# A seven-product down projection whose weight sums are made by adding DMAs

## What is computed

```python
h = _rmsnorm(x, norm_mlp[l])
u = jax.nn.relu(jnp.einsum('bsd,df->bsf', h, w_up[l]))      # (1, 256, 8192)
x = x + jnp.einsum('bsf,fd->bsd', u * u, w_down[l])         # (1, 256, 2048)
return _rmsnorm(x, norm_final)
```

## Time and profile before

| what | us |
|---|---|
| median of 3 runs | 1001.91 (1000.73 to 1002.18) |
| the profiled execution's own time | 1000.99 |
| its span in the trace | 999.2 |
| PE busy | 986.5 |
| DVE busy | 586.4 |
| ACT busy | 419.6 |
| packets of the main DMA queue, as a share of 16 engines | 52.1% |
| data moved | 193.52 MB |

### The profile page before, as it was taken

How to read it: one execution, slowest core, us unless ns; L and a number is a source line. 1 busy time by engine, 2 the same in 40 slices (tenths; PEclk the granted TensorE clock), 3 DMA queues, 4 the chain that set the end, 5 groups by cost and what they waited for, 6 DMA issues and landing times.

```text
span 999.2 us, 12457 instructions
## 1 busy us (share of the span) xinstructions
PE 986.5 (99%) x5088; PEld 847.2 (85%) x5088; DVE 586.4 (59%) x428; ACT 419.6 (42%) x325; POOL 1.4 (0%) x9
## 2 busy tenths in 40 slices
PE   8999999999999999999999999999999999999996
PEld 7888888888888888888888888888888888888885
DVE  6597777655554766544656654556565445656453
ACT  6644435354443434333444433343433334444342
POOL 0000000000000000000000000000000000000000
PEclk9999999999999999999999999999999999999998
DMA  9956543555544655555455455545545554555512
GB/s 327 392 194 229 190 188 122 215 211 190 189 169 169 233 189 195 183 208 177 165 211 206 176 203 191 187 151 213 209 183 207 176 204 132 211 209 205 187 66 84
DMA packets 29694, 193.52 MB, mean 194 GB/s; under 512 B 3296, under 2 KB 3552, under 8 KB 7136
## 3 DMA queue, kind: packets, MB, share of 16 engines
q1 hardware_dynamic: 29232, 190.85, 52.1%
q10 hardware_dynamic: 288, 1.18, 0.3%
q0 software_dynamic: 144, 1.05, 0.3%
HBM read 190.97 MB, written 2.10 MB: 193 GB/s over the span
## 4 chain that ended last, share of the span: by engine, by line
PE 94%; DMA 3%; SPq 1%; DVE 1%; ACT 0%; issue 0%; ACTq 0%
PE ps L343 44%; PE ps L252 33%; PE ps L255 17%; DMA w_raw<-w_stream 3%; SPq L208 1%; PE ps L277 0%; PE ps L329 0%; SPq L193 0%; DVE w_lo L628 0%; ACT w_hi L449 0%; PE ps L317 0%; DVE val L635 0%; PE ps L276 0%; PE ps L279 0%; ACT cross L483 0%
## 5 line engine op out<-in xcount | busy, mean ns | idle before, releaser
L628 DVE TENSOR_TENSOR w_lo<-w_raw,w_hi 128x2048 fp32r<-128x2048 f32 x172 | 392.0, 2291 | 280.4 <-ACT w_hi L449 279.7
L449 ACT ACTIVATE w_hi<-w_raw 128x2048 fp32r<-128x2048 f32 x172 | 326.8, 1912 | 344.0 <-PE ps L343 210.8
L252 PE MATMUL ps<-act_a,w_hi 128*128 128x512 f32 x1472 | 351.1, 391 | 0.0
L343 PE MATMUL ps<-w_hi,act_b 128*128 128x512 f32 x1280 | 345.3, 390 | 0.0
L252 PEld LDWEIGHTS ps<-act_a,w_hi 128*128 128x128 f32 x1472 | 271.0, 188 | 52.5
L343 PEld LDWEIGHTS ps<-w_hi,act_b 128*128 128x128 f32 x1280 | 239.8, 188 | 49.3
L343 PE MATMUL ps<-w_lo,act_b 128*128 128x512 f32 x640 | 199.7, 389 | 0.0
L255 PEld LDWEIGHTS ps<-act_a,w_lo 128*128 128x128 f32 x1472 | 188.6, 191 | 7.0
L255 PE MATMUL ps<-act_a,w_lo 128*128 128x256 f32 x1472 | 191.1, 283 | 0.0
L343 PEld LDWEIGHTS ps<-w_lo,act_b 128*128 128x128 f32 x640 | 120.2, 188 | 25.0
L635 DVE TENSOR_TENSOR val<-ps,cross 128x1024 f32<-128x1024 f32 x26 | 31.8, 1223 | 47.2 <-ACT cross L455 47.2
(11 more groups left out here) (68 smaller groups left out, 164.3 us busy)
## 6 DMA issues: line engine op xcount, KB each, us to landing
w_raw<-w_stream SPq DMA_DIRECT2D x172, 1024.0 KB, 4.8
w_raw<-w_stream SPq DMA_DIRECT2D x16, 256.0 KB, 7.9
x<-x_rows SPq DMA_DIRECT2D x2, 1024.0 KB, 17.4
mix_mem<-x_t SPq DMA_DIRECT2D x3, 512.0 KB, 8.2
out<-x SPq DMA_DIRECT2D x6, 256.0 KB, 2.7
mix_mem<-pool_w ACTq DMA_DIRECT2D x1, 1024.0 KB, 9.1
mix_mem<-g_final POOLq DMA_DIRECT2D x1, 1024.0 KB, 5.0
out<-val SPq DMA_DIRECT2D x2, 256.0 KB, 2.1
```

The lines of the kernel that those rows point to most:

```text
L252: return pe.matmul(ps[:, bank, :], weights_hi, act, start=first, stop=False)
L343: mm = pe.matmul(ps[:, NT * parity + t, :], a[:, at:at + P], cols, start=first and i == 0, stop=last and i == 2)
L449: act.activation(w_hi[:, c, :], w_raw[:, c, :], ACT.Copy).then_inc(hi_ready, 1)
L628: dve.tensor_tensor(out=w_lo[:, c, :], in0=w_raw[:, c, :], in1=w_hi[:, c, :].bitcast(F32), op=ALU.subtract)\
```

## The change

The row blocks of w_down are replaced by a scheme in the manner of Strassen, with seven block products in place of eight. The 8192 features are cut into 8 slices of 1024, each slice into two groups of 512. For one slice and one half of the output columns (1024 of 2048), activations are a 2 x 2 arrangement of quadrants (two token halves by two feature groups, A11, A12, A21, A22), and the weights another (four quadrants of 512 x 512, each one chunk of 1 MiB). Such a pair is a **unit**, d = 0 to 13; it does seven products of 128 tokens x 512 features x 512 columns, each with 12 matmuls. Some operands are sums of quadrants:

- Sums of activation quadrants (S5, N6, N3, S7) are made by DVE, once for a slice, that is for two units, and are then split into hi and lo by ACT and DVE (`quad_hi`, `quad_lo`).
- Four weight operands are sums (T1 to T4). T1, T2 and T4 are built one upon another in a buffer `sums[d % 2]` in `mix_mem`: SP loads quadrant 1, then POOL issues a DMA that adds quadrant 0 (T1), later quadrant 3 (T2), later quadrant 2 (T4). T3 is made in `w_raw` slot 3 by an adding DMA of quadrant 1 upon quadrant 3, after DVE has split quadrant 3. Each add is issued when DVE has split the sum before it.
- The running product sums lie in PSUM banks 4, 5 and 6, and DVE adds or subtracts them into `x` seven times per unit (`fold`, 128 x 512 each).

From the third up block on (t = 2 to 15, d = t - 2) PE does one up block and one unit, interleaved in a **step** of 11 items: up 0, A11·B11, S5·T1, up 1, N3·B22, N6·T2, up 2, S7·T3, up 3, A12·B21, A22·T4. They are called items 0 to 10 below. All up blocks from t = 2 use banks 0 to 3. The last slice is done plainly, with eight products for each half of the columns' pair (`plain`, 8 chunks of 24 matmuls). w_up blocks keep two `w_raw` slots, the quadrants the two others; `w_hi` and `w_lo` are rings of four slots over all items.

The core of the diff (hunks and lines left out are marked "..."):

```diff
+LEAD = 2
...
+UP_AT = (0, 3, 6, 8)
+A11_B11, S5_T1, N3_B22, N6_T2, S7_T3, A12_B21, A22_T4 = 1, 2, 4, 5, 7, 9, 10
+STEPS = 11
...
+PLAINS = 8
...
+FOLDS = 7
...
+        sums = (mix_mem[:, 0:CHUNK_W], mix_mem[:, CHUNK_W:2 * CHUNK_W])
...
+            def load_up(t, c, before):
+                sp.wait_ge(lo_ready, before + 1)
+                sp.dma_start(w_raw[:, c % 2, :], w_stream[CHUNKS * (FIRST_UP + t) + c, :, :])\
+                  .then_inc(raw_loaded[c % 2], 16)
+            def load_quad(to, d, n, before, loaded):
+                sp.wait_ge(lo_ready, before + 1)
+                sp.dma_start(to, w_quads[4 * d + n, :, :]).then_inc(loaded, 16)
+            sp.wait_ge(value_ready, 2)
+            for t in range(LEAD, UPS):
+                d = t - LEAD
+                lead = d == 0
+                load_quad(sums[d % 2], d, 1, up_item(1, 0) if d < 2 else term_item(d - 2, A22_T4),
+                          sum_base_loaded[d % 2])
+                load_up(t, 0, up_item(1, 0) if lead else up_item(t - 1, 2))
+                load_quad(w_raw[:, 3, :], d, 3, up_item(1, 3) if lead else term_item(d - 1, S7_T3),
+                          raw_loaded[3])
+                load_up(t, 1, up_item(1, 1) if lead else up_item(t - 1, 3))
+                load_quad(w_raw[:, 2, :], d, 0, up_item(1, 2) if lead else term_item(d - 1, A12_B21),
+                          raw_loaded[2])
+                load_up(t, 2, up_item(t, 0))
+                load_quad(w_raw[:, 2, :], d, 2, term_item(d, A11_B11), raw_loaded[2])
+                load_up(t, 3, up_item(t, 1))
...
+            def add_quad(to, d, n, after, added):
+                pool.wait_ge(lo_ready, after + 1)
+                pool.dma_start(to, w_quads[4 * d + n, :, :], accum_op=ALU.add).then_inc(added, 16)
+            def add_to_base(d):
+                pool.wait_ge(sum_base_loaded[d % 2], 16 * (d // 2 + 1))
+                pool.dma_start(sums[d % 2], w_quads[4 * d, :, :], accum_op=ALU.add).then_inc(t1_added, 16)
+            add_to_base(0)
+            for d in range(SEVENS):
+                add_quad(sums[d % 2], d, 3, term_item(d, S5_T1), t2_added)
+                add_quad(w_raw[:, 3, :], d, 1, term_item(d, N3_B22), t3_added)
+                if d + 1 < SEVENS:
+                    add_to_base(d + 1)
+                add_quad(sums[d % 2], d, 2, term_item(d, N6_T2), t4_added)
...
+            def term(d, which, quad, bank, first):
+                g = term_item(d, which)
+                pe.wait_ge(quad_ready, quad_count(d // 2, quad))
+                pe.wait_ge(hi_ready, g + 1)
+                to = ps[:, bank, :]
+                for k in range(CK):
+                    pe.matmul(to, quads[:, quad, k, 0:P], weights_of(w_hi, g, k),
+                              start=first and k == 0, stop=False, skip_group_check=not first)
+                    pe.matmul(to, quads[:, quad, k, P:2 * P], weights_of(w_hi, g, k),
+                              start=False, stop=False, skip_group_check=not first)
+                pe.wait_ge(lo_ready, g + 1)
+                for k in range(CK):
+                    mm = pe.matmul(to, quads[:, quad, k, 0:P], weights_of(w_lo, g, k),
+                                   start=False, stop=k == CK - 1, skip_group_check=not first)
+                mm.then_inc(chunk_used, 1)
+            for t in range(LEAD, UPS):
+                d = t - LEAD
+                up_chunk(t, 0)
+                if d == 0:
+                    pe.wait_ge(summed, turn(FIRST_UP) + LEAD)
+                else:
+                    pe.wait_ge(folded, FOLDS * d)
+                term(d, A11_B11, A11, NT, True)
+                term(d, S5_T1, S5, NT + 1, True)
+                up_chunk(t, 1)
+                pe.wait_ge(folded, FOLDS * d + 2)
+                term(d, N3_B22, N3, NT + 1, False)
+                term(d, N6_T2, N6, NT, False)
+                up_chunk(t, 2)
+                pe.wait_ge(folded, FOLDS * d + 4)
+                term(d, S7_T3, S7, NT, False)
+                up_chunk(t, 3)
+                term(d, A12_B21, A12, NT + 2, True)
+                pe.wait_ge(folded, FOLDS * d + 5)
+                term(d, A22_T4, A22, NT, False)
...
+                up_hi(t, 0)
+                take_up(t - 1)
+                act.wait_ge(raw_loaded[2], 16 * (FIRST_UP + LEAD + 2 * d + 1))
+                hi_of(term_item(d, A11_B11), w_raw[:, 2, :])
+                square_up(t - 1)
+                act.wait_ge(t1_added, 16 * (d + 1))
+                hi_of(term_item(d, S5_T1), sums[d % 2])
+                if folding:
+                    act.wait_ge(part_ready, parts + 1)
+                    quad_hi(s, S5, part_0, S5_T1)
+                up_hi(t, 1)
+                if folding:
+                    act.wait_ge(part_ready, parts + 2)
+                    quad_hi(s, N6, part_1, N6_T2)
+                act.wait_ge(raw_loaded[3], 16 * (FIRST_UP + LEAD + d + 1))
+                hi_of(term_item(d, N3_B22), w_raw[:, 3, :])
+                if folding:
+                    act.wait_ge(part_ready, parts + 3)
+                    quad_hi(s, N3, part_0, N3_B22)
+                    parts += 3
+                act.wait_ge(t2_added, 16 * (d + 1))
+                hi_of(term_item(d, N6_T2), sums[d % 2])
+                if folding:
+                    act.wait_ge(squared, t)
+                    quad_hi(s, A12, val[:, :, 0:P], A12_B21)
+                    quad_hi(s, A22, val[:, :, P:S], A22_T4)
+                else:
+                    act.wait_ge(squared, t)
+                    quad_hi(s + 1, A11, held[:, :, 0:P], A11_B11)
+                up_hi(t, 2)
+                act.wait_ge(t3_added, 16 * (d + 1))
+                hi_of(term_item(d, S7_T3), w_raw[:, 3, :])
+                up_hi(t, 3)
+                act.wait_ge(raw_loaded[2], 16 * (FIRST_UP + LEAD + 2 * d + 2))
+                hi_of(term_item(d, A12_B21), w_raw[:, 2, :])
+                act.wait_ge(t4_added, 16 * (d + 1))
+                hi_of(term_item(d, A22_T4), sums[d % 2])
...
+                if d:
+                    fold(d - 1, 5, S7_T3, NT, 1, 1, ALU.subtract)
+                if folding:
+                    quad_lo(s, S7, part_2)
+                up_lo(t, 0)
+                add_up(t - 1)
+                lo_of(term_item(d, A11_B11), w_raw[:, 2, :])
+                dve.wait_ge(squared, t)
+                if folding:
+                    made(dve.tensor_tensor(out=part_0, in0=val[:, :, P:S], in1=held[:, :, P:S],
+                                           op=ALU.subtract))
+                if d:
+                    fold(d - 1, 6, A12_B21, NT + 2, 0, 0, ALU.add)
+                lo_of(term_item(d, S5_T1), sums[d % 2])
+                if folding:
+                    quad_lo(s, S5, part_0)
+                    made(dve.scalar_tensor_tensor(out=part_1, in0=held[:, :, 0:P], scalar=-1.0,
+                                                  in1=part_0, op0=ALU.mult, op1=ALU.subtract))
+                if d:
+                    fold(d - 1, 7, A22_T4, NT, 1, 0, ALU.add)
+                up_lo(t, 1)
+                if folding:
+                    quad_lo(s, N6, part_1)
+                    made(dve.scalar_tensor_tensor(out=part_0, in0=part_1, scalar=-1.0,
+                                                  in1=val[:, :, 0:P], op0=ALU.mult, op1=ALU.subtract))
+                elif s + 1 < SLICES - 1:
+                    make_s7()
+                lo_of(term_item(d, N3_B22), w_raw[:, 3, :])
+                if folding:
+                    quad_lo(s, N3, part_0)
+                fold(d, 1, A11_B11, NT, 0, 0, ALU.add)
+                lo_of(term_item(d, N6_T2), sums[d % 2])
+                if folding:
+                    quad_lo(s, A12, val[:, :, 0:P])
+                    quad_lo(s, A22, val[:, :, P:S])
+                else:
+                    quad_lo(s + 1, A11, held[:, :, 0:P])
+                fold(d, 2, S5_T1, NT + 1, 1, 1, ALU.subtract)
+                up_lo(t, 2)
+                lo_of(term_item(d, S7_T3), w_raw[:, 3, :])
+                fold(d, 3, N3_B22, NT + 1, 0, 1, ALU.subtract)
+                up_lo(t, 3)
+                fold(d, 4, N6_T2, NT, 0, 1, ALU.subtract)
+                lo_of(term_item(d, A12_B21), w_raw[:, 2, :])
+                lo_of(term_item(d, A22_T4), sums[d % 2])
```

More of the change, by code:

```diff
@@ new lines, in plain @@
+            def plain(f, halves, done):
+                g = FIRST_PLAIN + f
+                d, k2, n = PLAIN_OF[f]
+                bank = (6, 4, 0, 2)[2 * d + n]
+                of_half = ((A11, A21), (A12, A22))[k2]
+                pe.wait_ge(hi_ready, g + 1)
+                pe.wait_ge(lo_ready, g + 1)
+                for k in range(CK):
+                    for i, (at, of) in enumerate(((0, w_hi), (P, w_hi), (0, w_lo))):
+                        for t in halves:
+                            mm = pe.matmul(ps[:, bank + t, :], quads[:, of_half[t], k, at:at + P],
+                                           weights_of(of, g, k), start=k2 == 0 and k == 0 and i == 0,
```

(49 more changed lines are left out.)

245 lines of the change are left out of this document (173 added, 72 removed).

## The result

| | before | after |
|---|---|---|
| median | 1001.32 us (4 runs) | 1108.98 us (4 runs, 1105.71 to 1112.98) |
| profiled execution, span | 999.2 us | 1111.2 us |
| mean granted TensorE clock | 0.996 | 0.958 |

The ratio is 1.108, 95% interval 1.103 to 1.112: 10.8% slower. I forecast 1014 us, 1.3% slower, with a range of 970 to 1058. The direction was right, the size was not, and the range missed.

The account below looks back on a forecast made before the run. PE was taken as the bound. From the profiled 1001.0 us, 38.1 us of removed matmuls came off and 14 units x 3.6 us of stalls (50.4) were added: 1013.3, with 0.9 for the median 1014 us; range 970 to 1058.

Parts of the forecast that it names:

- Removed work: w_down products on PE: 168 fewer matmuls at 0.2268 us each save 38.1 us, all on the path.
- ACT, DVE: Added work in a 41.3 us step: ACT 27 us, hidden by PE; DVE 38.7 (even units) and 33.9 (odd).
- DVE's crowd: DVE's queue before item 4: fold 2 makes it 1.3 us late in even units, 9 us in all.
- The price of an add: Each adding DMA reads twice: 5.2 us of the engines, 7.4 us alone; T2 9.3 us with nearby loads.
- The queue of POOL: POOL issues T2, T3, next T1, T4; only adds queue behind its waits, and the base is asked for before T4.
- the T4 chain: T3, next T1 and T4 one behind another, sharing engines with four plain loads: item 10 late, 1.1 us a unit.
- Start and end at zero: First up blocks, first unit's lead-in, plain slice and last block add nothing; without their cover 1 to 2 us.
- Slow adding: Rival: addition holds the engines for 3 or 4 loads' time, DMA is the bound: 1114 or 1259 us; chance 0.14.
- Cheap adds: Rival: an add flows like a plain load, T2 lands in 5 us, only DVE's crowd is left: 973 us; chance 0.26.

Follow-up runs that it names:

- adds as cheap as loads: Changed kernel with the four adding DMAs of a unit made plain loads of the same bytes, so the sums are not formed: 987.4 us, ratio 0.987.
- the base early: Changed kernel with SP's load of the next sum base moved ahead of three other loads, order of adds kept: 1036.5 us, ratio 1.036.
- both queue edits: Changed kernel with the next sum base loaded earlier and T4's add issued before the next unit's T1 add: 1031.7 us, ratio 1.031.
- small adds: Changed kernel with each adding DMA covering only 128 of the 2048 columns, order and waits kept: 987.8 us, ratio 0.987.
- The best version that keeps the whole computation: Changed kernel with sum base loaded early, T4 issued before next T1, and the last unit's folds 6 and 7 done first at the end: 1027.0 us, ratio 1.027.
- a control fills a wait with work: Changed kernel with 16 small unused matmuls of ones ahead of PE's wait for item 10: 1111.5 us against 1109.0.

## Why the prediction was wrong

**Removed work: right.** 168 matmuls are gone, and with adds as cheap as loads the kernel does get faster, 987 us.

**ACT, DVE: right in kind.** DVE's crowd was laid out within 0.6 us, and costs 3.4 us for the 9. ACT was busy 521 us, never the bound.

**The price of an add: right.** 5.3 us of the engines for a forecast 5.2; 8.2 us at the fastest for 7.4; T2 8.7 us for 9.3.

**The queue of POOL: the step that failed.** I wrote that POOL's adds stand behind its waits only, and of the wait for the next base that it "is asked for after lo3 and T4 only after lo5", and took this for harmless. Measured, the base takes 13.6 us to land (median), issued into T2's traffic, and POOL stands 5.8 to 12.9 us there after T3; T1 then goes in front of T4, and T4 lands 17.7 us after its issue (median, 19.6 in the step shown). In the T4 chain I counted T1 ahead of T4 but let T1 start at once behind T3. The result is a step of 51.3 us for 44.9. With the base early the step is 45.5 us, with both queue edits 45.1, about what the forecast's sum said, and the kernel 1031.7. Part of that agreement is luck: with both edits T4 is no longer late, and the charge of 1.1 us for it stands in for other queueing that I had not priced.

**Start and end at zero: wrong.** I looked at the last block and not at the join of the units and the plain slice, where PE waits 10.2 us for fold 6 behind the last up result on DVE. And item 4 of the first unit waits 5.9 us with the queues mended, 3.7 even with small adds. I had named 1 to 2 us for lost cover. The forecast's 1014, with 0.2 us more in each of 14 units and these two waits, makes 1033; the kernel with both queue edits took 1031.7.

**The rivals.** Slow adding was given 1114 us for an add of three loads' engine time. The time came out near that number, but not by that mechanism: the add is 1.9 times a load. The DMA share of 0.85 in the steps, below the 0.94 of the kernel with both queue edits, tells the two apart: an engine that is the bound has no room. Cheap adds at 973 would have been 987.

**What did not beat the kernel before.** The best version that keeps the whole computation takes 1027.0 us. With all adds in it the engines need 43.4 us a step, and before a pair of blocks took 44.0 us of PE, so at most some 8 us were to be had with the engines never idle. Whether seven products on every second slice only, where the adds would have twice the time, beats 1001 us was not tried.

## What to carry to other kernels

When a DMA depends on another DMA's landing, look at what stands behind its wait in the same queue, and give the transfer that is due first the first place; two lines were worth 53 us here, one load issued earlier 72, and both together 77. Price a DMA's latency in the traffic it is issued into, not from the trace's quiet median: 4.8 us became 13.6. And when a control fills a wait with work, look whether the filling outlasts the wait: here it did in ten units of fourteen, and the control said nothing. A saving on a nearly saturated engine is worth no more than the spare of the resource that pays for it, 2.7 us of PE against 43.4 of 44 us of DMA.

## What the runs showed of the hardware

- An adding DMA of 1 MiB from HBM into SBUF takes 5.3 us of the 16 engines, a plain one on the same queue 2.8; the fastest add of the changed kernel landed in 8.2 us, the fastest of all kernels here in 7.7.
- A POOL tensor addition of 128 x 2048 float32 takes 4.7 to 5.0 us here, and a DVE operation with two SBUF inputs that starts beside it lasts until it is over: 4.87 us for 0.69. Folds with one PSUM input kept their 0.68 us.
- Issuing an adding DMA holds POOL 0.86 us, and DVE's subtractions did not get longer beside it (2.29 us before and after).
- A 64 KB add sent right behind a 1 MiB add on POOL's queue landed in 11.6 us (median), one sent with nothing just ahead of it in 2.6.
- After a wait of 4.47 us the granted clock in PE's next 12 matmuls was 0.61, and they took 4.4 us in place of 2.7. What this costs in a kernel where PE is not the bound is not shown here.
